# ScalarE's order in an attention block: both exponentials ahead of the square, the copy and the turned probabilities

## The reference

```python
for i in range(S // Q_BLOCK):            # 8 blocks of 128 queries
    s = einsum('bqhmd,bkhmd->bhmqk', q[:, q0:end], k[:, :end]) * scale   # m = 0, 1
    s = where(rel >= 0, s + bias, -inf)
    p = softmax(s, axis=-1)
    a = p[:, :, 0] - lam * p[:, :, 1]
    outs.append(einsum('bhqk,bkhv->bqhv', a, v[:, :end]))
```

## Time and profile before

| what | value |
|---|---|
| median of 3 runs | 2839.43 us (2838.8 to 2844.62) |
| the profiled execution | 2840.74 us, of which the span of its instructions is 2838.9 us |
| TensorE, matmuls busy | 2627.0 us, 93% of the span |
| VectorE busy | 1156.0 us, 41% |
| ScalarE busy | 826.9 us, 29% |
| GpSimd busy | 139.7 us, 5% |
| mean granted TensorE clock | 0.964 of full speed |

### The profile page before, as it was taken

The page is one execution under the profiler, slowest core; times in us unless marked ns, Lnnn a source line. Parts: engine busy times, 40 slices in busy tenths (PEclk is TensorE's granted clock), DMA queues, the critical chain, the costliest instruction groups (busy, mean ns, idle before and its releaser), DMA issues. The chain is left out here.

```text
span 2838.9 us, 30677 instructions
## 1 busy us (share of the span) xinstructions
PE 2627.0 (93%) x12450; PEld 2122.9 (75%) x12450; DVE 1156.0 (41%) x1839; ACT 826.9 (29%) x1463; POOL 139.7 (5%) x165
## 2 busy tenths in 40 slices
PE   8799879879999999999999996896999999999997
PEld 7578757658788888878767884674878888887875
DVE  0556345555433321135662454556531111113544
ACT  0422234444211111134552123444431111113433
POOL 0001100002000000001010010000200000000000
PEclk9999989989999999999999998997999999999998
DMA  5252110012444411144341112000321111114443
GB/s 196 83 189 86 31 37 23 16 52 97 153 137 133 141 50 48 46 147 165 132 165 52 38 38 45 23 16 25 110 73 52 45 52 45 52 45 141 171 146 136
DMA packets 183992, 243.61 MB, mean 86 GB/s; under 512 B 9531, under 2 KB 141484, under 8 KB 182828
## 3 DMA queue, kind: packets, MB, share of 16 engines
q1 hardware_dynamic: 172556, 200.74, 22.3%
q0 software_dynamic: 11296, 40.92, 4.2%
HBM read 224.05 MB, written 17.58 MB: 85 GB/s over the span
## 5 line engine op out<-in xcount | busy, mean ns | idle before, releaser
L1710 PE MATMUL ps<-hT,wsp 128*128 128x512 f32 (+1 forms) x2080 | 830.3, 399 | 49.3 <-DVE F L1337 39.6
L1712 PE MATMUL ps<-hT,wsp 128*128 128x512 f32 (+1 forms) x2080 | 815.9, 392 | 0.0
L1711 PE MATMUL ps<-hT,wsp 128*128 128x512 f32 (+1 forms) x2080 | 815.3, 392 | 0.0
L1077 DVE TENSOR_TENSOR wsp<-raw,wsp 128x1024 fp32r<-128x1024 f32 (+2 forms) x140 | 168.0, 1200 | 867.4 <-ACT wsp L638 698.6
L1710 PEld LDWEIGHTS ps<-hT,wsp 128*128 128x128 f32 (+1 forms) x2080 | 390.2, 188 | 156.9 <-issue 65.0
L1712 PEld LDWEIGHTS ps<-hT,wsp 128*128 128x128 f32 (+1 forms) x2080 | 389.9, 187 | 88.2 <-issue 1.9
L1711 PEld LDWEIGHTS ps<-hT,wsp 128*128 128x128 f32 (+1 forms) x2080 | 390.4, 188 | 81.3 <-issue 2.0
L638 ACT ACTIVATE wsp<-raw 128x1024 fp32r<-128x1024 f32 x84 | 89.1, 1060 | 778.5 <-PE ps L1712 615.7
L2035 PE MATMUL ps<-hT,asp 128*128 128x512 f32 x1032 | 251.4, 401 | 16.5 <-DVE asp L1608 16.3
L2035 PE MATMUL ps<-wsp,asp 128*128 128x512 f32 x1080 | 255.3, 393 | 4.0 <-DVE asp L1608 3.7
L2035 PEld LDWEIGHTS ps<-hT,asp 128*128 128x128 f32 x1032 | 197.9, 193 | 64.7 <-DVE hT L1600 12.0
(11 more groups left out here) (189 smaller groups left out, 2513.4 us busy)
## 6 DMA issues: line engine op xcount, KB each, us to landing
raw<-in_w_down SPq DMA_DIRECT2D x132, 512.0 KB, 3.5
raw<-in_w_gate_up SPq DMA_DIRECT2D x88, 512.0 KB, 3.8
F<-in_w_mod SPq DMA_DIRECT2D x80, 512.0 KB, 4.7
raw<-in_w_in SPq DMA_DIRECT2D x48, 512.0 KB, 3.8
out_x<-W POOLq DMA_DIRECT2D x32, 512.0 KB, 3.4
W<-out_x POOLq DMA_DIRECT2D x24, 512.0 KB, 5.5
raw<-in_w_out SPq DMA_DIRECT2D x16, 512.0 KB, 3.4
F<-in_w_mod SPq DMA_DIRECT2D x6, 1024.0 KB, 18.8
```

The source lines that it names most:

```text
L1077: v.tensor_tensor(wsp[0:np_, r, 1, 0:w], raw[0:np_, r, 0:w], wsp[0:np_, r, 0, 0:w].bitcast(F32), ALU.subtract).then_inc(s_lo, 1)
L1710: mm(o, a(0), b(0), start=start, stop=False)
L1711: mm(o, a(0), b(1), start=False, stop=False)
L1712: return mm(o, a(1), b(0), start=False, stop=stop)
```

## The change

Three lines of ScalarE's list move up in every iteration of `head(h)`: the exponential of map 1 of the next block now stands directly behind that of map 0, ahead of `outs` and `probs(b, 0)`. No instruction is added or removed, and nothing changes on the other engines.

```diff
@@ -888,15 +888,15 @@
                             exps(h, b + 1, 0)
                         elif h < HEADS - 1:
                             exps(h + 1, 0, 0)
+                        if b < NT - 1:
+                            exps(h, b + 1, 1)
+                        elif h < HEADS - 1:
+                            exps(h + 1, 0, 1)
                         if b:
                             outs(h, b - 1)
                         elif h:
                             outs(h - 1, NT - 1)
                         probs(b, 0)
-                        if b < NT - 1:
-                            exps(h, b + 1, 1)
-                        elif h < HEADS - 1:
-                            exps(h + 1, 0, 1)
                         if b >= 4:
                             probs(b, 1)
```

## The result

The change makes the kernel a little slower: 2846.72 us against 2841.46 us (medians of 20 runs each), a ratio of 1.0017 with a 95% interval of 1.001 to 1.0024, that is +2.8 to +6.8 us. The two intervals overlap at about +3 us, and the forecast was +2.8. Gains and losses in us are from here on the ratio's, times the time of before, which need not be the difference of the two medians. One of the 11 executions of a later kernel (everything but head 1, b = 6) took 3881.01 us at a granted clock of 0.643 and is in none of the ratios.

A forecast was written before the change was run, and what follows sets the result against it. TensorE's work and gaps were taken to bound the kernel, but ScalarE's list in head 3. Per layer -1.76 + 3.18 = +1.42 us, twice +2.8, on 2839.43 gave 2842.2 us, range 2836 to 2849.

The forecast's parts named there:

- the sum: Both attention stages: per layer -1.76 us in heads 0 to 2 and +3.18 in head 3, +1.42; both layers +2.8.
- Heads 0 to 2 lose their gaps before the scores: Gains per layer: head 0, b = 2 -0.39 us; head 0, b = 3 -1.46; heads 1 and 2, b = 3 together -0.94.
- Head 1, b = 6 loses: Second transposes wait for the later exponential and copies, so the scores come later: +1.03 us per layer.
- The nine covered iterations cost nothing: Heads 0 to 2, b of 4 or more with `fill`: nine dense matmuls hide the later `probs(b, 0)`; nothing taken.
- Head 0, b = 6 and 7: No `fill` between the transposes, but long `weighted` products cover the second exponential: nothing, upper bound 0.31 us.
- Head 3 is bound by the end of ScalarE's list: Head 3, per layer: what counts is when ScalarE ends its list, not when the scores may start; sum +3.18 us.
- The strict order of ScalarE's queue: On ScalarE everything behind a waiting instruction waits too; if later ones could pass, the losses would be nothing.
- The clock as a rival: Longer gaps ending head 3 keep TensorE at 1.2 GHz, also in matmuls behind: 2847 to 2849 us, chance 0.22.
- A gain by sooner scores: Head 3's path through the scores: 2833.6 us, chance 0.08; or all 22 gaps before scores shrink: 2822, chance 0.03.

The follow-up runs named there:

- everything but head 1, b = 6: The whole change against the kernel before, but head 1, b = 6 keeps the old order: 2841.26 us, ratio 1.0002.
- head 3 alone: New order in head 3 only, heads 0 to 2 as in the kernel before: 2848.07 us, ratio 1.002.
- b = 5 and 6 alone: New order only in head 3, b = 5 and 6, the rest as in the kernel before: 2847.68 us in one execution.
- filling the idle 0.4 us in b = 1 to 3: Kernel before, but in head 3, b = 1 to 3 square and copy stand between the two exponentials: 2837.92 us in one execution.
- a choice by place: New order in heads 0 to 2 except head 1, b = 6, and at head 3, b = 0; else as before: 2836.3 us, ratio 0.998.

## Why the prediction was right

The forecast was +2.8 us, within what a measurement tells from no change. Measured were +4.8 and +0.6, the first with an interval that reaches down to the forecast and not to zero, the second with the forecast inside. The mechanism was right, and part of the closeness of the number is luck. The steps that the sum names come to +1.0 us in the first layer and +1.5 in the second, for +1.42. What it left out is -0.7 and +0.4, and it is so small only because the stretch at head 2 (+1.6) and the rest (-2.2 and -1.2) nearly cancel. Nor do the two layers repeat each other, as the sum had them: the stages are 0.33 and 1.93 us longer. Point by point:

- *Heads 0 to 2 lose their gaps before the scores.* Right in place and size: each gain came within 0.2 us. The largest, head 0, b = 3, gave 1.56 to 1.65 for 1.46, though 0.27 us of its gap is left in the first layer. Where the excess comes from is open: the same step moved by -0.61 to +0.18 us in the kernels that kept the old order there.
- *Head 1, b = 6 loses.* Right: +0.98 for +1.03, and gone when that iteration kept its order.
- *The nine covered iterations cost nothing.* Right: in the changed kernel no wait for L883 shows in them. Head 0, b = 6 and 7, were put at nothing as well. By that step the first exponential of head 1 comes 0.17 to 0.21 us sooner in the ten stages that have the new order there, and stays within 0.04 us in all others; whether the kernel keeps it isn't shown. (The table `STEPS` has no `fill` in three iterations of head 0, b = 2, 3 and 7, and not in four.)
- *Head 3 is bound by the end of ScalarE's list.* Right, and shown from three sides: head 3 alone is slower by 5.7 us, b = 5 and 6 alone carry 2.9 us in the second layer, and filling the idle 0.4 us in b = 1 to 3 removes the loss of five of those six iterations and part of the sixth. Between the two exponentials ScalarE stands idle for 0.28 us at b = 2 and 0.40 at b = 6, for the 0.4 or little less of the prediction.
- *The strict order of ScalarE's queue*, the rule that spoke against the change, holds in every row above. No copy passed an exponential that waited.
- *The clock as a rival.* The sum held no term for it. It moved more than I allowed for and in both directions: +1.6 us a layer at the start of head 2, up to -1.1 at the start of the stage and at that of head 1. The piece at the start of the stage isn't the change's own, since nothing that was moved stands ahead of it, and it differs from -1.06 to +0.35 us between executions. Those at head 1 and head 2 go with the shift that the new order makes, as the table under "Everything but head 1, b = 6" shows, so they are probably in part the change's own; no run separates the two. It was not the dense matmuls behind the stage, where I looked for it: in the 6 us behind the last square the granted clock is 0.98 and 0.99, 1.00 before.
- *A gain by sooner scores* (2822 or 2833.6) was excluded by head 3 alone: there they came sooner after b = 0 to 3, and the time went up.

## What to carry to other kernels

An instruction moved up on an in-order engine does not start sooner than its input, and everything that it passed now waits with it. Ask what else that engine could do until the input comes, and keep just so much in front: here 0.4 us, a square and a copy. Ask also what the moved instruction used to lie over: the exponential had covered the transposes between two copies, and in b = 5 and 6 the idle wait and the lost cover together cost 1.1 to 2.0 us an iteration, of which the wait is some 0.4. And judge each place by its own path: the same edit gained in the heads where TensorE was the path and lost in the head where ScalarE was, so that a choice by place (5.7 us faster) beats both uniform orders.

## What was not expected of the hardware

At the start of head 2 nine matmuls instead of fifteen fitted into the same stretch, at a granted clock of 0.54 instead of 1.00, behind the same instructions of TensorE and the same wait of 1.96 us. It was so in 13 of the 14 stages that ran at least 0.8 us ahead of before's times at that place, with the old order there or the new one, and in none of the six that ran within 0.5 us of them. Each time it cost 1.4 to 1.6 us. So a stage that gains time in one head may give it back to the clock in the next. Differences of a few microseconds between profiles of this kernel are of that size, so single executions had to be compared by stages and steps.
